# A decoder block kernel: the projections to u and v as seven half-size products each

## What is computed

```python
h = rms_norm(x, g_mix)                       # x: 512 x 1024
z = h @ w_in                                 # w_in: 1024 x 4800
u, v, q_lat, kv_lat, k_rope, gate_a, gate_b = split(z)   # 1024, 1024, 384, 256, 64, 1024, 1024
y_a = spatial_gating(gelu(u), gelu(v), ...)  # LayerNorm of gelu(v), 128x128 mixing in chunks
y_b = mla_attention(q_lat, kv_lat, k_rope, ...)
x = x + (sigmoid(gate_a) * y_a + sigmoid(gate_b) * y_b) @ w_o
x = x + moe(rms_norm(x), ...)                # 64 experts, top 8, one shared expert
x = x + sigmoid(rms_norm(x) @ w_ple_gate) * rms_norm(p @ w_ple_proj)
```

## Time and profile before

| | |
|---|---|
| median of three runs | 1110.98 us |
| the profiled execution | 1110.49 us |
| its span | 1108.7 us |
| TensorE busy | 1092.9 us, 99% |
| VectorE busy | 861.2 us, 78% |
| ScalarE busy | 787.0 us, 71% |
| GpSimd busy | 423.6 us, 38% |
| start to the end of the first latent chunk | 0 to 30.66 us |
| second latent chunk | to 44.72 us |
| v and u, four chunks | to about 131.8 us |
| gates, four chunks | to 219 us |

### The profile page before, as it was taken

One profiled execution on the slowest core, in us unless ns is written; L12 is line 12 of the kernel. 1 busy time (PEld: TensorE's weight loads), 2 busy tenths in 40 slices (PEclk: granted clock), 3 DMA queues, 4 the chain that ended last, 5 costly groups with the idle time before them and its releaser, 6 DMA issues.

```text
span 1108.7 us, 17836 instructions
## 1 busy us (share of the span) xinstructions
PE 1092.9 (99%) x5488; PEld 914.7 (83%) x5488; DVE 861.2 (78%) x1239; ACT 787.0 (71%) x1270; POOL 423.6 (38%) x477
## 2 busy tenths in 40 slices
PE   7999999999999999999999999999999999999998
PEld 7988888878778888888888888888888888888787
DVE  4535532278765468999999999999999999999865
ACT  6644433357654343888888898889888988888772
POOL 1120000015276003355556555555655555555400
PEclk9999999999999999999999999999999999999999
DMA  7422422112402259999999999999999999999632
GB/s 251 153 76 76 142 85 76 29 57 71 158 1 71 101 225 381 356 377 382 394 393 388 391 393 388 391 391 393 395 396 396 396 394 393 392 393 359 192 151 76
DMA packets 72130, 291.60 MB, mean 263 GB/s; under 512 B 15187, under 2 KB 20598, under 8 KB 47126
## 3 DMA queue, kind: packets, MB, share of 16 engines
q1 hardware_dynamic: 52672, 254.13, 57.3%
q0 software_dynamic: 18768, 34.79, 12.5%
q10 hardware_dynamic: 646, 2.12, 0.5%
HBM read 284.61 MB, written 42.07 MB: 295 GB/s over the span
## 4 chain that ended last, share of the span: by engine, by line
PE 93%; DVE 3%; ACT 2%; POOL 1%; issue 1%; DMA 0%; ACTq 0%; POOLq 0%; DVEq 0%
PE bank L2065 11%; PE bank L2067 11%; PE bank L2066 11%; PE bank L1752 7%; PE bank L1789 6%; PE bank L1793 6%; PE bank L1790 6%; PE bank L2093 5%; PE bank L2091 5%; PE bank L2092 5%; PE bank L2030 5%; PE bank L1743 2%; PE bank L1944 1%; PE bank L2163 1%; PE bank L2165 1%; PE bank L2164 1%
## 5 line engine op out<-in xcount | busy, mean ns | idle before, releaser
L1624 DVE TENSOR_TENSOR arena_r<-arena,win_r 128x1024 fp32r<-128x1024 f32 x252 | 292.0, 1221 | 21.9 <-ACT win_r L1082 19.1
L1082 ACT ACTIVATE win_r<-arena 128x1024 fp32r<-128x1024 f32 x252 | 246.5, 1069 | 0.5 <-DMA resid<-in_w_exp_up 0.5
L2065 PE MATMUL bank<-win_r,work_r 128*128 128x512 f32 x512 | 206.5, 403 | 0.6 <-issue 0.6
L2066 PE MATMUL bank<-win_r,x_low_r 128*128 128x512 f32 x512 | 199.5, 390 | 0.0
L2067 PE MATMUL bank<-arena_r,work_r 128*128 128x512 f32 x504 | 197.4, 392 | 0.0
L1604 DVE TENSOR_TENSOR arena_r<-arena,hT_r 128x1024 fp32r<-128x1024 f32 x128 | 150.5, 1217 | 0.5 <-ACT hT_r L1090 0.5
L733 POOL DMA_INDIRECT moe_sum<-ya,sidx x64 | 111.5, 1743 | 102.7 <-ACT ya L1118 86.0
L1789 PE MATMUL bank<-arena_r,hT_r 128*128 128x512 f32 (+2 forms) x320 | 121.9, 381 | 2.2 <-DVE win_r L1222 2.1
L1790 PE MATMUL bank<-arena_r 128*128 128x512 f32 (+2 forms) x320 | 121.1, 378 | 0.0
L1793 PE MATMUL bank<-win_r,hT_r 128*128 128x512 f32 (+2 forms) x320 | 121.0, 378 | 0.0
L2067 PEld LDWEIGHTS bank<-arena_r,work_r 128*128 128x128 f32 x504 | 94.6, 188 | 21.7
(11 more groups left out here) (321 smaller groups left out, 2213.4 us busy)
## 6 DMA issues: line engine op xcount, KB each, us to landing
arena<-in_w_exp_down SPq DMA_DIRECT2D x64, 1024.0 KB
arena<-in_w_exp_gate SPq DMA_DIRECT2D x63, 1024.0 KB
arena<-in_w_exp_up SPq DMA_DIRECT2D x63, 1024.0 KB
win<-in_w_in SPq DMA_DIRECT2D x8, 2048.0 KB, 7.8
win<-in_w_o SPq DMA_DIRECT2D x2, 2048.0 KB, 7.9
arena<-in_w_ple_gate SPq DMA_DIRECT2D x2, 2048.0 KB, 13.7
arena<-moe_sum SPq DMA_DIRECT2D x7, 512.0 KB, 7.0
win<-in_mla_w_qb SPq DMA_DIRECT2D x4, 576.0 KB, 4.0
```

The source lines that it names most:

```text
L1082: act.activation(gu_hi[n % 2][:, :, cols], raw[:, :, cols], ACT.Copy).then_inc(gu_hi_r, 1)
L1624: dve.tensor_tensor(low_[:, :, cols], raw[:, :, cols], gu_hi[n % 2][:, :, cols].bitcast(F32), ALU.subtract).then_inc(gu_lo_r, 1)
L2065: pe.matmul(b_, x_hi[:, k, :], w_hi, start=(k == 0), stop=False)
L2066: pe.matmul(b_, x_lo[:, k, :], w_hi, start=False, stop=False)
```

## The change

For v, and then for u, the 512 x 1024 by 1024 x 1024 product is made of seven products of half size in each direction (256 tokens, 512 channels, 512 columns) instead of eight. A product is 2 tiles x 4 steps x 3 matmuls = 24 matmuls, named 11, T1, T2, 21, 22, T3, T4. Their left sides are blocks of the rows or the sums S1 to S4 of blocks, their right sides blocks of the weights or sums of blocks T1 to T4.

- Row sums: VectorE makes S1 to S4 once (`row_combos`, twelve operations), ScalarE and VectorE split each into high and low; both projections use them.
- Weight sums: T1 to T4 are built in SBUF by eight transfers on GpSimd's queue that add a 1 MB block of w_in onto what lies there (`add_weights`). T1, T2 and T4 are built in the same place, one after the other, each when the low part of the one before has been taken; each transfer also waits for the one before it.
- Results: VectorE adds the products into v or u (`add_products`, 14 operations of 128x512 for each), ScalarE copies the first product out (`first_product_out`) and applies gelu in SBUF, when a block is complete, with the norm's factor.
- The gain g_mix goes on the rows: the evacuation of the transposed tiles multiplies by it, in 128x128 operations, four for each half tile on ScalarE and VectorE each. The weight splits no longer scale and take two k at a time.
- Places: v's and u's weights lie in ya, in the residual's place (x is overwritten after its transposes and loaded again ahead of the chunk w = 8), and in the two win buffers. The ln gains are loaded after product 21 of u.
- Order: the angles, latent norms and LayerNorm move from the v/u stage into the gate chunks. On VectorE `row_combos` comes after the last `h_evac` and ahead of `split(1)`.

The core of the diff (indentation reduced):

```diff
+PRODUCTS = ("11", "T1", "T2", "21", "22", "T3", "T4")
+PRODUCT_ROW = {"T1": "S1", "T2": "S2", "22": "S4", "T3": "S3"}
+PRODUCT_BANK = {"11": 0, "T1": 4, "T2": 2, "21": 6, "22": 0, "T3": 4, "T4": 6}
+HIGHS = (("11", "S1", "S2", "T1", "S3", "S4", "T2", "21", "22", "T3", "T4"), ("11", "T1", "T2", "21", "22", "T3", "T4"))
+LOWS = (("11", "S1", "T1", "S2", "S3", "S4", "T2", "21", "22", "T3", "T4"), ("11", "T1", "T2", "21", "22", "T3", "T4"))
...
+    def pairs_loads():
+        sp.wait_ge(tr_done, 2 * NT)
+        sp.wait_ge(rms_sq, NT)
+        half_load(v2(xr_, 0, HK, 512), half_chunk(0, "11"), ld_w0[0], 32)
+        free(0)
+        half_load(v2(win0, 0, HK, 512), half_chunk(0, "22"), win_ready[0], 32)
+        half_load(v2(win0, 2 * D, HK, 512), half_chunk(0, "21"), win_ready[1], 32)
+        free(1)
+        half_load(v2(win1, 2 * D, HK, 512), half_chunk(1, "22"), win_ready[1], 48)
+        sp.wait_ge(accumulated, 32)
+        half_load(v2(xr_, 2 * D, HK, 512), half_chunk(1, "11"), ld_w0[0], 48)
+        half_load(v2(win1, 0, HK, 512), half_chunk(1, "12"), ld_w0[1], 48)
+        sp.wait_ge(pj_done, products_done(0, "21"))
+        half_load(v2(win0, 2 * D, HK, 512), half_chunk(1, "11"), win_ready[0], 48)
+        sp.wait_ge(pj_done, products_done(0, "22"))
+        half_load(v2(win0, 0, HK, 512), half_chunk(1, "21"), ld_mix, 48)
+        sp.wait_ge(pj_done, products_done(1, "21"))
         sp.dma_start(lng, bc(a["sgu_ln_g"][0], D)).then_inc(ld_ln, 16)
         sp.dma_start(lnb, bc(a["sgu_ln_b"][0], D)).then_inc(ld_ln, 16)
...
         if w == 2:
+            half_load(v2(ya_, 0, HK, 512), half_chunk(0, "11"), ld_mix, 32)
+            half_load(v2(ya_, 2 * D, HK, 512), half_chunk(0, "12"), ld_w0[1], 32)
             small_loads()
+            pairs_loads()
+        if 2 <= w < 6:
+            continue
+        if w == 8:
+            sp.wait_ge(pj_done, products_done(1, "T4"))
+            for t in range(NT):
+                rows_of_x(t)
...
+    def add_weights(n, dst, p, name):
+        if n > 1:
+            pool.wait_ge(accumulated, 16 * (n - 1))
+        pool.dma_start(dst, half_chunk(p, name), accum_op=ALU.add).then_inc(accumulated, 16)
+    def sum_in_place(p):
+        return v2(xr_, p * 2 * D, HK, 512)
+    pool.wait_ge(ld_w0[0], 32)
+    add_weights(1, sum_in_place(0), 0, "12")
+    pool.wait_ge(ld_w0[1], 32)
+    add_weights(2, v2(ya_, 2 * D, HK, 512), 0, "22")
+    pool.wait_ge(lo_ready, split_count(LOWS, 0, "T1"))
+    add_weights(3, sum_in_place(0), 0, "22")
+    pool.wait_ge(lo_ready, split_count(LOWS, 0, "T2"))
+    add_weights(4, sum_in_place(0), 0, "21")
...
-            act.activation(hT_hi[:, 4 * (T % 2):4 * (T % 2) + 4, t * P:(t + 1) * P],
-                           bank[4 + T % 2][:, :].rearrange("p (k q) -> p k q", k=4), ACT.Copy).then_inc(hT_hi_ready, 1)
-
-    def split(w):
+            for i in range(4):
+                k = 4 * (T % 2) + i
+                last = act.activation(hT_hi[:, k, t * P:(t + 1) * P], bank[4 + T % 2][:, i * P:(i + 1) * P],
+                                      ACT.Copy, scale=gmix[:, k:k + 1])
+            last.then_inc(hT_hi_ready, 1)
...
+            act.activation(whi_r[:, ks, 0:n], v2(win[w % 2], 0, KD, n)[:, ks, :], ACT.Copy).then_inc(hi_ready, 2)
...
+    def first_product_out(p):
+        act.wait_ge(pj_done, products_done(p, "11"))
+        for i in range(2):
+            act.activation((vbuf, ya)[p][:, i, 512:D], bank[i][:, :], ACT.Copy).then_inc(pj_free[i], 2)
...
+    split(1)
+    evac(0, NT - 1)
+    for t in range(NT):
+        act.wait_ge(pj_free[t], 1)
+    high_part(0, "11")
+    high_part(0, "S1")
+    evac(1, 0)
+    high_part(0, "S2")
+    high_part(0, "T1")
+    evac(1, 1)
+    high_part(0, "S3")
+    high_part(0, "S4")
+    evac(1, 2)
+    evac(1, 3)
+    act.wait_ge(whi_used, 2 * KD)
+    high_part(0, "T2")
+    high_part(0, "21")
+    first_product_out(0)
+    high_part(0, "22", products_done(0, "T1"))
+    high_part(0, "T3", products_done(0, "T2"))
+    high_part(0, "T4", products_done(0, "T2"))
+    gelu(0, "11")
+    high_part(1, "11", products_done(0, "21"))
+    gelu(0, "12")
+    high_part(1, "T1", products_done(0, "22"))
+    gelu(0, "22")
+    gelu(0, "21")
+    first_product_out(1)
+    high_part(1, "T2", products_done(0, "T4"))
+    high_part(1, "21", products_done(1, "T1"))
+    high_part(1, "22", products_done(1, "T1"))
+    high_part(1, "T3", products_done(1, "T2"))
+    high_part(1, "T4", products_done(1, "T2"))
+    gelu(1, "11")
...
+            for i in range(4):
+                k = 4 * half + i
+                last = dve.scalar_tensor_tensor(LO_OF[k][:, q], bank[4 + T % 2][:, i * P:(i + 1) * P], gmix[:, k:k + 1],
+                                                hT_hi[:, k, q].bitcast(F32), ALU.mult, ALU.subtract)
             last.then_inc(tr_free[T % 2], 1)
...
+    def row_combos():
+        first, second, upper, lower = slice(0, HT), slice(HT, SEQ), slice(0, HK), slice(HK, KD)
+        lo_ = {k0: z for k0, _, z in hT_lo}
+        def hi(ks, q):
+            return hT_hi[:, ks, q].bitcast(F32)
+        def lo(k0, q):
+            return lo_[k0][:, :, q].bitcast(F32)
+        for i in range(2):
+            dve.wait_ge(tr_free[i], NT)
+        S1, S2, S3, S4 = (s_raw[n] for n in ("S1", "S2", "S3", "S4"))
+        def lower_lo(z, q, op):
+            link(dve.tensor_tensor(z[:, 0:2, :], z[:, 0:2, :], lo(4, q), op))
+            return dve.tensor_tensor(z[:, 2:4, :], z[:, 2:4, :], lo(6, q), op)
+        dve.tensor_tensor(S3, hi(upper, first), hi(upper, second), ALU.subtract)
+        link(dve.tensor_tensor(S1, hi(lower, second), hi(upper, second), ALU.subtract))
+        link(dve.tensor_tensor(S2, lo(0, first), lo(0, second), ALU.subtract))
+        link(lower_lo(S1, second, ALU.add))
+        dve.tensor_tensor(S1, S1, lo(0, second), ALU.subtract).then_inc(combined, 1)
+        dve.tensor_tensor(S3, S3, S2, ALU.add).then_inc(combined, 1)
+        dve.wait_ge(combined, 2)
+        link(dve.tensor_tensor(S4, S1, lo(0, first), ALU.add))
+        dve.tensor_tensor(S2, S4, hi(upper, first), ALU.add).then_inc(combined, 1)
+        dve.wait_ge(combined, 3)
+        link(dve.tensor_tensor(S4, S2, hi(lower, first), ALU.subtract))
+        lower_lo(S4, first, ALU.subtract).then_inc(combined, 1)
...
+    def low_part(p, name, room=None):
+        if room is not None:
+            dve.wait_ge(pj_done, room)
+        if name[0] == "S":
+            dve.wait_ge(hi_ready, split_count(HIGHS, p, name))
+            dve.tensor_tensor(s_lo[name], s_raw[name], s_hi[name].bitcast(F32), ALU.subtract).then_inc(lo_ready, 1)
+            return
+        for part in range(2):
+            dve.wait_ge(hi_ready, split_count(HIGHS, p, name, part))
+            dve.tensor_tensor(B_LO[p][name][part][1], B_RAW[p][name][part][0], B_HI[p][name][part][1].bitcast(F32),
+                              ALU.subtract).then_inc(lo_ready, 1)
...
+            if quad == "X":
+                dve.wait_ge(pj_free[i], 4 + 2 * p)
+                dve.tensor_tensor(C21, b_, C12, ALU.subtract).then_inc(pj_free[2 + i], 2)
+                continue
+            if quad == "Y":
+                dve.wait_ge(pj_free[2 + i], 4 + 2 * p)
+                last = dve.tensor_tensor(C22, C21, b_, ALU.subtract)
+            elif quad == "11":
+                last = dve.tensor_tensor(C11, b_, C12, ALU.add)
+            elif quad == "12":
+                read("11")
+                last = dve.tensor_tensor(C12, C22, b_, ALU.subtract)
+            elif quad == "22":
+                read("12")
+                last = dve.tensor_tensor(C22, C22, b_, ALU.subtract)
+            elif quad == "W":
+                read("Y")
+                last = dve.tensor_tensor(C21, b_, C21, ALU.subtract)
+            else:
+                read("W")
+                last = dve.tensor_tensor(C21, b_, C21, ALU.add)
+            last.then_inc(sum_read, 1)
...
+    row_combos()
     split(1)
+    low_part(0, "11")
+    low_part(0, "S1")
+    low_part(0, "T1")
+    low_part(0, "S2")
+    low_part(0, "S3")
+    low_part(0, "S4")
+    low_part(0, "T2")
+    low_part(0, "21")
+    low_part(0, "22")
+    add_products(0, "X")
+    add_products(0, "Y")
+    low_part(0, "T3")
+    low_part(0, "T4")
+    add_products(0, "11")
+    add_products(0, "12")
+    low_part(1, "11")
+    add_products(0, "22")
+    add_products(0, "W")
+    low_part(1, "T1", products_done(0, "T3"))
+    add_products(0, "21")
...
+    def product(p, name):
...
+        if row is not None and p == 0:
+            pe.wait_ge(lo_ready, split_count(LOWS, 0, row))
...
+            for k in range(HK):
+                if i == 0 and k % 2 == 0:
+                    pe.wait_ge(lo_ready, split_count(LOWS, p, name, k // 2))
+                if row is not None:
+                    a_hi, a_lo = s_hi[row][:, k, tok(i)], s_lo[row][:, k, tok(i)]
+                else:
+                    k_, q = (k if name == "11" else k + HK), tok(i + 2 if name == "T4" else i)
```

(60 more changed lines are left out.)

206 lines of the change are left out of this document (144 added, 62 removed).

## The result

The changed kernel takes 1118.86 us (median of four runs, 1117.69 to 1119.16) against 1110.92 for the kernel before beside it: a ratio of 1.007, 95% interval 1.0055 to 1.0085. It is slower by 7.9 us, 6.3 more than the forecast of 1112.6. Its profiled execution took 1119.16 us with a span of 1117.1.

A forecast was written before the change was run, and what follows sets the result against it. The prediction took TensorE's own time to bound the kernel. Its terms, -10.9 + 1.6 + 9.1 + 1.9 + 0.4 = +2.1 us on 1110.5, gave 1112.6 us, with an 8 in 10 range of 1107.5 to 1121.

The forecast's parts named there:

- What bounds the kernel: Whole kernel: TensorE, busy for 99% of the span, is the bound; a change pays only through TensorE's own time.
- The matmuls, -10.9: v/u stage: 336 matmuls instead of 384, 48 removed at 0.2267 us each, -10.9 us.
- The start: First latent chunk: small evacuations with the gain on the rows make it end later, +1.6 us, bounds +0.7 and +2.6.
- The row sums: Before the second latent chunk: row_combos takes 12.5 us on VectorE ahead of split(1), leaving TensorE idle for +9.1 us.
- The clock: Second latent chunk: after the 9 us of idleness some 13 matmuls run at the 1.2 GHz level, +1.9 us.
- rival C: Second latent chunk: the clock does not fall in the 9 us of idleness; 1110.7 us, chance 0.10.
- The weight sums: Products of v and u: adding transfers of 9.2 us each, hidden for v, +0.4 us at u's T2.
- Rival B: Products of v and u: the adding transfers become the bound; 1117.9 us at 12 us a transfer, chance 0.26.
- What was at nothing: Products and gate chunks: additions, splits, moved angles and norms, and extra loads are all covered, at no cost.
- D: Before the second latent chunk: the row sums do not hold TensorE up; 1101.6 us, chance 0.12.
- E: Products: something in the chain of reused places costs one product's time, 5.4 us; 1118 us, chance 0.10.
- The forecast's own range: Whole kernel: case A, the forecast, by the bounds of start, row sums and clock; 1110.8 to 1114.5 us, chance 0.42.

The follow-up runs named there:

- after with the one swap: The changed kernel with split(1) put ahead of row_combos on VectorE: 1119.75 us, ratio 1.0083 to the kernel before.

## Why the prediction came out as it did

- **What bounds the kernel.** Right. TensorE's own time and what it waits for account for all but 1.0 us of the difference, and that 1.0 is within the spread of the traces (below).
- **The matmuls, -10.9.** Right in size: TensorE is busy for 76.5 us in the product stage, where 336 x 0.2267 = 76.2. With the 1.1 of wait that stage holds, 9.5 arrived.
- **The start, +1.6, measured +5.7: this is the step that failed.** The small operations cost what was said. The first matmul was to come 1.1 us later and came 3.1 later: the chain from the first evacuation to it took 4.43 us instead of 2.92 (+1.5 for the 1.1), and the evacuation itself began 1.6 later. Of that 0.2 is the transposes' own start (4.51 for 4.29), the rest the table load, which the prediction doesn't mention, as it doesn't mention the wait for the gain. Then the prediction let slack take up most of the first matmul's delay (tile 1 at +1.5) and let tiles 2 and 3 follow at TensorE's pace. Nothing took it up: tile 1's transposes came 3.1 later, its matmuls 4.5, and tiles 2 and 3 added 0.4 and 0.6, since each tile's chain of evacuations starts only when its transposes are there. The slow pitch of the first matmuls is no part of it: it ends 4.4 us behind the first one before, 4.6 after. The upper bound given, +2.6, was less than half of what came.
- **The row sums, +9.1, measured 9.14.** Right in size and place: 12.6 us on VectorE for 12.5. But "this is the step on which the sign hangs" is wrong. Without that wait the kernel is no faster; the sums of the weights took its place.
- **The clock, +1.9, measured +2.2.** Right, and rival C falls. The granted clock between 45.5 and 50 us was 0.50, the 1.2 GHz level, with a pitch of 0.27 for 320 columns. The Trainium skill's page "TensorE: Matmul & The Clock Gate", "Part 1: The HAM clock gate", has this right for the 9 us; what shorter waits did is below.
- **The weight sums, 9.2 us each and +0.4.** Measured 9.6 (median; three of eight over 10) and +1.1. The scatter of before was the right row to size it by. The +0.4 came close in part by offsetting errors: u's T2 landed in 8.5, 0.7 less than taken, but T1's low part ended 1.0 later behind the start of the products than said (38.8 us for 37.8), and the issue and the split added some 0.5. The Trainium skill's page "Collectives: The Full Stack", "Why ReduceScatter is half of AllGather", says that a transfer that adds moves at half the rate; the engine share of 40.9% against 20.6% for the same bytes agrees. Rival B was priced as an extra on top of the forecast. It is not one: the chain of sums and the row sums run side by side and only the later of the two is paid, so B's 5.3 us was hidden below A's 9.1 and came out when A's was removed (7.8 at v's T2, 2.2 at u's).
- **What was at nothing.** Right: VectorE is busy for 44.8 of 77.6 us in the product stage, 51.4 of 87.1 in the gates (24.5 + 25 = 49.5 forecast), and the first gate chunk starts without a wait.
- **Rivals D and E.** Both fall as mechanisms. The row sums held TensorE up for all of 9.1 us, and no reused place cost a product.
- **Open.** The last 1.0 us lies behind the gates, in two short waits that the profile puts down to issue. It need not be the change's: from the end of the gates to the end of the span the twelve traces of this case take 889.1 to 891.1 us, and after with the one swap 889.1 against 890.7 for after. It was not tried whether VectorE could start on each small evacuation while ScalarE makes the next.

The sum by the measured terms is -10.9 + 5.7 + 9.1 + 2.2 + 1.1 + 0.3 (the rest of the product stage) - 0.2 (gates) + 1.0 (behind them) = +8.3; the spans differ by 8.4. The time of 1118.86 is inside the range given, 1107.5 to 1121. That it lies inside is in part luck. The forecast's own range, 1110.8 to 1114.5, was missed, and "no change" with it; the upper part of the wide range had been drawn for rivals B and E (1117.9 and 1118), and what filled it was the start. Of the chances, by their own working, slower should have had 0.465 and faster 0.12, for the 0.44 and 0.14 given.

## What to carry to other kernels

A saving on the bounding engine is a budget for what feeds that engine: here 10.9 us of matmuls were spent on a start that had become serial (5.7) and a burst on VectorE that nothing covered (11.3 with its clock), and they showed only when the feeding was put in order. Two limits that run side by side don't add: before a wait is called the price of a change, ask which date is second latest, since that is what its removal gives. And where loads and a chain of dependent transfers share the DMA engines, issue each by when it is needed: holding back 2 MB was worth 5.5 us with the clock that came back, more than any edit on an engine.

## What the runs showed of the hardware

- A transfer that adds 1 MB onto SBUF landed in 9.6 us (median), a plain one in 5.6, and it took twice the engines' time. One that stood 3.3 us behind another of its kind, beside 4 MB of other loads, took 20 us; with 2 MB of these held back it took 15.
- Which wait costs TensorE its clock did not follow the wait's length alone: after 3.67 us the granted clock stayed at 1.00, after 3.84, 3.72 and also 2.93 us (three other kernels) it was at 0.50. The slow pitch behind these three lasted for 13, 7 and 8 matmuls. Nor is it fixed by the kernel: the one with the 3.67 us had a mean clock below 1.00 in its six executions without a trace, and the one with the 2.93 us had 0.998 in two executions and 0.999 or 1.000 in nine. What else enters in was not tested.
- The first matmuls' slow pitch did not end at a fixed distance: in two kernels whose first matmul stood at 9.63 and 9.73 it ended 4.9 and 2.7 us later. Differences of 1 us at a start may come from that alone.
- ScalarE's first table load ran at 3.79 us, ahead of its activation's wait, where that activation had one wait (for the transposes), and at 5.71, when the transposes had come, where a wait for the gain stood in front of it. Why was not tested. A one-column activation ahead of both brought the load back to 3.78 and the first matmul forward by 1.4 us.
